# The two gate products of a decoder trunk: eight block products each before, seven after, with weight sums put aside in DRAM

## The reference, cut to what matters

```
hid  = square(relu(x @ ffn_w1[i]))
x    = layer_norm(ALPHA * x + hid @ ffn_w2[i], ln2_g[i], ln2_b[i])
gate = sigmoid(x @ ple_gate_w[i])          # 1024x1024 @ 1024x1024
x    = x + gate * (p[i] @ ple_w[i])        # 1024x256  @ 256x1024
```

## Time and profile before

| | |
|---|---|
| three runs, median (lowest to highest) | 2071.39 us (2070.79 to 2071.64) |
| the profiled execution, its own time | 2070.66 us |
| its span in the profile | 2068.9 us |
| PE busy | 2052.1 us (99%) |
| DVE, ACT, POOL busy | 1325.2, 853.9, 790.2 us |
| mean granted TensorE clock | 0.999 |
| moved by DMA | 306 MB, 148 GB/s |

### The profile page before, as it was taken

One profiled execution on the slowest core, in us unless ns is written; L12 is line 12 of the kernel. 1 busy time (PEld: TensorE's weight loads), 2 busy tenths in 40 slices (PEclk: granted clock), 3 DMA queues, 4 the chain that ended last, 5 costly groups with the idle time before them and its releaser, 6 DMA issues. The chain is left out here.

```text
span 2068.9 us, 25147 instructions
## 1 busy us (share of the span) xinstructions
PE 2052.1 (99%) x9437; PEld 1702.7 (82%) x9437; DVE 1325.2 (64%) x1677; ACT 853.9 (41%) x1241; POOL 790.2 (38%) x523
## 2 busy tenths in 40 slices
PE   9999999999999999999999999999999999999999
PEld 9888788888888888888878887888888888888887
DVE  4744775655666757564687769775655666666563
ACT  3112465454544334431433334655445543334430
POOL 5212157787702000212266751167877412000220
PEclk9999999999999999999999999999999999999999
DMA  5111123444589655411022238034444599554221
GB/s 189 42 62 45 38 82 137 144 161 156 197 309 390 218 201 182 141 34 41 21 88 86 87 133 299 1 122 145 150 158 142 205 382 362 185 202 153 97 87 41
DMA packets 190708, 306.05 MB, mean 148 GB/s; under 512 B 13472, under 2 KB 71932, under 8 KB 190588
## 3 DMA queue, kind: packets, MB, share of 16 engines
q1 hardware_dynamic: 189888, 304.14, 42.1%
q10 hardware_dynamic: 700, 0.31, 0.1%
HBM read 233.62 MB, written 70.78 MB: 147 GB/s over the span
## 5 line engine op out<-in xcount | busy, mean ns | idle before, releaser
L1326 POOL TENSOR_TENSOR w_lo<-raw,w_hi 128x512 fp32r<-128x512 f32 x92 | 131.0, 1455 | 744.0 <-ACT w_hi L1441 744.0
L1339 POOL TENSOR_TENSOR op_lo<-op_sum,op_hi 128x512 fp32r<-128x512 f32 x151 | 225.1, 1506 | 34.4 <-ACT op_hi L1643 28.5
L1608 ACT CAST hop_hi<-h_raw 128x1024 fp32r<-128x1024 f32 x124 | 130.4, 1051 | 257.0 <-PE bank_a L2367 155.4
L1643 ACT CAST op_hi<-op_sum 128x512 fp32r<-128x512 f32 x151 | 93.9, 622 | 329.5 <-POOL op_sum L1420 87.9
L2365 PE MATMUL bank_a<-wop_hi,hop_hi 128*128 128x512 f32 x576 | 224.2, 389 | 4.7 <-DVE resid L2153 4.7
L2131 DVE TENSOR_TENSOR hop_lo<-h_raw,hop_hi 128x1024 fp32r<-128x1024 f32 x124 | 152.0, 1226 | 117.5 <-ACT hop_hi L1608 117.3
L2367 PE MATMUL bank_a<-wop_hi,hop_lo 128*128 128x512 f32 x576 | 224.1, 389 | 0.0
L2366 PE MATMUL bank_a<-wop_lo,hop_hi 128*128 128x512 f32 x576 | 224.1, 389 | 0.0
L1339 POOL TENSOR_TENSOR op_lo<-w_raw,op_hi 128x512 fp32r<-128x512 f32 x115 | 164.2, 1428 | 116.4 <-ACT op_hi L1643 115.3
L2367 PE MATMUL bank_a<-xt_hi,op_lo 128*128 128x512 f32 x456 | 177.4, 389 | 0.0
L2365 PE MATMUL bank_a<-xt_hi,op_hi 128*128 128x512 f32 x456 | 177.4, 389 | 0.0
(11 more groups left out here) (243 smaller groups left out, 4879.4 us busy)
## 6 DMA issues: line engine op xcount, KB each, us to landing
w_raw<-in_ffn_w_dram SPq DMA_DIRECT2D x144, 512.0 KB, 6.8
h_raw<-h_spill SPq DMA_DIRECT2D x112, 512.0 KB, 5.2
h_spill<-h_tile SPq DMA_DIRECT2D x170, 256.0 KB, 2.1
w_raw<-in_ffn_w_dram SPq DMA_DIRECT2D x112, 256.0 KB, 3.3
w_raw<-in_od_w_in_dram SPq DMA_DIRECT2D x40, 256.0 KB, 3.3
w_raw<-in_od_w_out_dram SPq DMA_DIRECT2D x18, 512.0 KB, 7.6
raw<-in_ple_gate_w_dram SPq DMA_DIRECT2D x32, 256.0 KB, 3.5
h_spill<-h_tile2t SPq DMA_DIRECT2D x28, 256.0 KB, 2.0
```

Of the source, the lines that this page charges most:

```text
L1326: pool.tensor_tensor(lo, raw[:, n % NRAW, :], hi.bitcast(F32), ALU.subtract).then_inc(lo_split, 1)
L1339: pool.tensor_tensor(by_four(op_lo[s]), operand_raw(tr, b, op), by_four(op_hi[s]).bitcast(F32), ALU.subtract).then_inc(op_low, 1)
L1608: act.copy(hop_hi[k][:, :, :], h_raw[a.hop_chunk(i)][:, :, :]).then_inc(ahead_hi, 1)
L1643: act.copy(by_four(op_hi[s]), operand_raw(tr, b, op)).then_inc(op_high, 1)
```

## The change

The 1024x1024 gate product is cut in quadrants: tokens by input channels (A11, A12, A21, A22), input by output channels (B11 to B22). With S1 = A21+A22, S2 = S1-A11, S3 = A11-A21, S4 = A12-S2 and T1 = B12-B11, T2 = B22-T1, T3 = B22-B12, T4 = T2-B21 there are seven products: m1 = A11 B11, m2 = A12 B21, m7 = S3 T3, m6 = S2 T2, m5 = S1 T1, m3 = S4 B22, m4 = A22 T4. Each is 4 token tiles of 12 matmuls. The four output quadrants are sums of them, partly formed by letting a product run on in the same bank, partly by an ACT copy and a DVE addition. `p @ W_p` keeps its count, in four quadrants of four tiles (6 matmuls each): one among m2's tiles, the others (`p12`, `p22`, `p21`) at the end.

The operands made of weights (B22, T3, T1, T2, T4) are formed in the MLP's second product, in stages `park` beside items 20 to 47: ACT issues DMA loads of the weight quadrants, POOL makes the four sums, ACT casts to hi, DVE subtracts to lo, ACT issues the DMAs that put both into DRAM (`gate_dram`). In the gate stage SP loads each operand (2 MB: hi and lo, 1 MB each) when the product before it in the same buffer is done. The operands made of tokens (S1 to S4, A22) are formed by DVE and ACT within the gate stage. p's transposes now all stand after item 53, and p's load after item 47.

```diff
+GATE_ITEMS = ("m1", "m2", "m7", "m6", "m5", "m3", "m4", "p12", "p22", "p21")
+PARKED = ("B22", "T3", "T1", "T2", "T4")
+PARK_FROM, PARK_STEPS = 20, 14
...
-            if i == LAST_FORM - PAIRS:
+            for m in range(2):
+                s = i - PARK_FROM - m * PARK_STEPS
+                if 0 <= s < PARK_STEPS:
+                    add("park", item=s, half=m, layer=layer)
+            if i == LAST_FORM:
                 add("p", layer=layer)
...
-            if i == LAST_FORM + 4:
-                add("turn_p", half=0, layer=layer)
             if i == LAST_FORM + 5:
                 add("second", layer=layer)
+                add("turn_p", half=0, layer=layer)
+                add("turn_p", half=1, layer=layer)
...
     (SP, the loads in the gate stage)
+                if name == "m1":
+                    gate_product_done(sp, st, "m1")
+                    part("T3", 0)
+                if name == "m2":
+                    sp.wait_ge(b_full, st.gb + HT + 1)
+                    part("T2", 1)
+                if name == "m7":
+                    gate_product_done(sp, st, "m7")
+                    part("T1", 0)
...
+                if name == "m6":
+                    gate_product_done(sp, st, "m6")
+                    part("B22", 1)
+                if name == "m5":
+                    gate_product_done(sp, st, "m5")
+                    part("T4", 0)
...
     (POOL, one of three places of park)
+                if st.item == 4:
+                    park_landed(pool, st, 3)
+                    park_done(pool, st, "T3r")
+                    step(park[1], park[1], park[2], ALU.subtract)
+                    park_done(pool, st, "T1r")
+                    step(park[2], park[0], park[2], ALU.add)
...
     (ACT, the loads and stores of park, first steps)
+                if s == 0:
+                    if m == 0:
+                        act.wait_ge(ahead_dve, ahead[layer].dve[3 * PAIRS - 1])
+                    else:
+                        park_stored(act, st, 0)
+                    quarter(1, 1, park[0])
+                    quarter(0, 1, park[1])
+                if s == 2:
+                    park_done(act, st, "B22l")
+                    store("B22", 2, 3)
+                if s == 3:
+                    park_stored(act, st, 1)
+                    quarter(0, 0, park[2])
...
     (DVE, the operands of tokens behind m2; pairs of 128x1024)
+                if name == "m7":
+                    gate_product_done(dve, st, "m2")
+                    x_step(g_part, xt12[0].bitcast(F32), g_sum[48], ALU.subtract, "S2r")
+                    gate_x_done(dve, layer, "S4a1")
+                    x_low(xt11[1], g_sum[48], xt11[0], "S2")
+                    x_step(g_sum[168], g_sum[168], g_sum[176], ALU.add)
...
+                    x_step(g_sum[56], g_part, xt12[1].bitcast(F32), ALU.add, "S4a")
+                    x_low(xt12[1], g_sum[56], xt12[0], "S4")
+                if name == "m6":
+                    gate_product_done(dve, st, "m7")
+                    x_low(s3[1], g_sum[168], s3[0], "S1")
+                    affine(range(HT, HT + 2))
...
     (PE, m1 with the second half's transposes within)
+                if name == "m1":
+                    pe.wait_ge(unit_lo, st.need_x[0])
+                    for k in range(HT):
+                        if k == HT - 1:
+                            turn_groups(st.inner[0], range(0, 4))
+                        gate_tile(k, free_bank("A", st, k)).then_inc(a_full, 1)
+                    turn_groups(st.inner[0], range(4, 8))
+                    return
...
+                if name[0] == "m":
+                    x_part, w_part = {"m7": ("S3l1", "T3"), "m6": ("S2l1", "T2"), "m5": ("S1l1", "T1"),
+                                      "m3": ("S4l1", "B22"), "m4": ("Xl1", "T4")}[name]
+                    gate_x_done(pe, layer, x_part)
+                    gate_part_landed(pe, layer, w_part)
+                    for k in range(HT):
+                        gate_tile(k, free_bank(ring, st, k)).then_inc(full, 1)
+                    return
```

More of the change, by code:

```diff
@@ L388, in make_plan, with slab_pieces @@
     ends = {}
+    def slab_pieces(slab):
+        return 6 if slab[0] == "gate" and slab[2] else 4
     def add(kind, slab=None, last=False, **args):
@@ L580, in gates @@
         add("more", slab=("gate", layer, 0), split_next=False, load_next=False)
[L581 to L598 removed]
+        first = add("gm", item=0, layer=layer)
+        gx = add("gx", source="ln", half=1, js=list(range(KT)), layer=layer, ln=2 * layer + 1, ring="B")
+        first.inner = [gx]
+        turned[1] = "gb", at["gb"]
+        items = [first]
+        for i in range(1, len(GATE_ITEMS)):
+            if GATE_ITEMS[i] == "p21" and layer == 0:
+                nested = turns("gate", 0, [0, 1, 2, 3], nested=True)
+            args = dict(slab=("gate", layer, 1)) if i == 1 else {}
+            items.append(add("gm", item=i, layer=layer, load_next=GATE_ITEMS[i] == "m4",
+                             split_next=GATE_ITEMS[i] == "p22", **args))
+            if GATE_ITEMS[i] in ("m4", "p22"):
+                slab_end.append(("gb", at["gb"]) if GATE_ITEMS[i] == "m4" else ("ga", at["ga"]))
+        if layer == 0:
+            items[-1].inner = [nested]
+            turns("gate", 0, [4, 5, 6, 7])
+        for st in items:
+            st.heads = {GATE_ITEMS[s.item]: s for s in items}
+            st.gx = gx
+        gx.heads = items[0].heads
     def short_conv():
@@ L944, in staged @@
         def staged(st, k):
[L946 removed]
+            early = st.source == "ln" and st.ln % 2 == 0 or st.source == "gate"
+            if st.kind == "turn" and st.source == "gate" and st.half == 0 and st.js[k] >= 4:
+                return g_turn[:, st.js[k] - 4, :]
             if st.kind == "turn" and early and st.js[k] < 4:
@@ L1301, in stage @@
                     load_gb(ln1_g[0], ln1_b[0], D)
-                if st.kind == "gate" and st.layer == 1:
-                    c = slice(st.col * HALF, (st.col + 1) * HALF)
-                    for k, t in enumerate(st.tiles):
-                        sp.wait_ge(x_new, st.xnew + k + 1)
-                        sp.dma_start(out_v[:, t, c], resid[:, t, c]).then_inc(out_done, 16)
             for st in plan:
@@ new lines, in gate_units @@
+            def gate_units(st):
+                act.wait_ge(unit_lo, st.unit)
+                for k, j in enumerate(st.js):
+                    act.wait_ge(b_full, st.gb + k + 1)
+                    g = ROW_G[1] + st.layer * KT + j
+                    b = ROW_B[1] + st.layer * KT + j
+                    act.activation(g_sum[168 if j < 4 else 176][:, j % 4, :], bank_b[(st.gb + k) % RING][:, :], ACT.Identity,
+                                   scale=cols[:, g:g + 1], bias=cols[:, b:b + 1]).then_inc(gate_turned, 1)
@@ L1555, in stage @@
                     split_high(st.cur + 1, st.piece, 4, end)
-                fifth = st.split_next and st.cur + 1 < n_slabs and slabs[st.cur + 1][0][0] == "gate"
                 if st.kind == "split":
@@ L2408, in stage @@
             def stage(st):
-                if st.first and st.cur > 0 and not (st.kind == "more" and slabs[st.cur][0][2] >= 2):
+                if st.first and st.cur > 0:
                     pe.wait_ge(lo_split, st.n("piece"))
```

502 lines of the change are left out of this document (376 added, 126 removed).

## The result

The changed kernel takes 2075.26 us (median of 20 runs, 2072.83 to 2080.68) against 2071.66 (20 runs, 2070.32 to 2073.14): ratio 1.0021, 95% interval 1.0014 to 1.0027. It is slightly slower; 2057.2 had been forecast, in a range up to 2067. The profiled execution took 2075.14 us, its span is 2073.6.

A forecast was written before the change was run, and what follows sets the result against it. PE, busy 99% of the span, was taken to bound the kernel: 21.8 us of matmuls saved less 7.6 us of new PE waits leaves 14.2, so 2057.2 us against 2071.39; range 2049.5 to 2067.

The forecast's parts named there:

- What bounds the kernel, and what goes: Whole kernel: PE, busy 99%, bounds it; 48 fewer gate matmuls a layer at 0.227 us save 21.8 us in both layers.
- Parking in the second product, "I take 0": MLP's second product, items 20 to 47: idle time and prepared items hide the parking steps, so PE loses 0 us.
- the prediction's own sign of it: MLP's second product: a stretch grown longer than 305 us would show the forecast wrong, parking not being hidden.
- four prepared items (21.8 us) between it and PE: MLP's second product: operands prepared four items ahead were counted as 21.8 us of cover for ACT's load and store waits.
- The port: MLP's second product: POOL's sums may each hold DVE 2.46 us on the shared port; DVE stays under 88 us, sum unchanged.
- Rival 3: MLP's second product: load and store round trips of 12.5 us outrun DVE's cover, 9.6 us reach PE, 2066.8; chance 0.15.
- Before m1: Ahead of the first gate product: the norm ends later, PE waits 0.3 us a layer, bounds 0 and 2.5.
- The gate stage: Gate stage, each layer: PE waits for DVE's low parts, 0.5 us for S2 ahead of m6, 2.0 for S1 ahead of m5.
- The weight operands: Gate stage: 2 MB loads land in about 10 us, shortest time allowed 10.9, so PE waits 0; bounds 7 and 19.
- rival 2: Gate stage: weight operands land late, at 19 us a part costing 14.2 us a layer, 2085.6; chance 0.09.
- The end of layer 0: Mixer's first product: POOL's splits slow three DVE additions by 0.9 us, so PE waits 1.5 us for xt_lo; bounds 0 and 5.
- The end of the program: After the last matmul: DVE's last two operations follow as before, plus 0.5 us.

The follow-up runs named there:

- e1: Changed kernel with every parking step cut to 128 of 1024 columns or 64 KB, gate-stage loads of parked operands too: 2057.47 us, ratio 0.9934 to before.
- e3: Changed kernel with DVE's five parking subtractions of each half cut to 128 of 1024 columns: 2059.16 us, ratio 0.9941 to before.
- e2: Changed kernel with only GpSimd's four parking sums of each half cut to 128 of 1024 columns: 2061.43 us, ratio 0.9951 to before.
- e10: Changed kernel with only the second half's parking begun at item 33 instead of 34: 2082.89 us, ratio 1.0050 to before.
- e11: Changed kernel with bank readings at items 24 and 48 earlier, second-half parking from item 33, sums on DVE, POOL's layer-0-end splits held back: 2056.74 us.
- e9: Changed kernel with DVE's bank readings at items 24 and 48 put ahead of one item's operand work: 2061.95 us, ratio 0.9946 to before.

## Why the prediction was wrong, step by step

- *What bounds the kernel, and what goes.* Right: PE, 96 matmuls, 0.227 us each, 21.8 us. e1 ends within 0.3 us of the forecast.
- *Parking in the second product, "I take 0".* **This step failed.** It measured 9.2 and 8.8 us, and the prediction's own sign of it came: a second product longer than 305 us, here 313.8. It set the new work against two covers: DVE's idle time (27 us a half) and "four prepared items (21.8 us) between it and PE". Both are true of the operands, and no operand was late. But the same queue holds the reading of m7's banks, which PE needs about an item after the bank is full and which has 0.5 us. The idle time in front of it was also no reserve: in the 52 us ahead of item 47 and up to the reading, before, DVE was idle 14.2 us, 5.8 for loads and 8.4 for ACT. Of this 6.3 was left afterwards, the last of it 16.9 us ahead of the reading. An average over 88 us did not tell that. Of the new work DVE's own subtractions (e3) and POOL's sums (e2) delay the reading; stores can too (e10), and what they cost in the changed kernel is open.
- *The port.* The prediction gave POOL's sums 2.46 us each and said that the sum does not change by them. They took 3.1 on average (group of instructions by line, which answers to the earlier trace rows),

```profile
L1477 POOL TENSOR_TENSOR park<-park,park 128x1024 f32<-128x1024 f32 x16 | 49.8, 3111 | 248.3 <-DMA park<-in_ple_gate_w_dram 142.1
```

  and of the 13 DVE instructions of 128x1024 that began while one ran, ten took 3.4 us instead of 1.22 and three 2.2 to 2.6. The Trainium skill, "SBUF — State Buffer", Who interferes with whom, has the rule (an exclusive lock between DVE and GpSimd); the trace agrees, 3.42 against 1.22 us. The prediction cited the rule and set it against the average over 88 us.
- *Rival 3, "parking is not hidden".* The right place and kind, at 0.15. Its size was wrong, 9.6 us in all against 18, as it too counted the lead of 21.8 us as cover, and nothing in it spoke of the clock (5.2 of the 18).
- *Before m1.* Forecast 0.3 a layer; PE waits for the norm in neither layer.
- *The gate stage.* The second wait, for S1, was forecast at 2.0 and measured 1.46; the first, for S2, at 0.5 and measured 0.29. Timeline of PE:

```profile
934.77 0.50 PE L2730 MATMUL bank_a<-w_hi,xt_hi 128*128 128x512 f32 x1 [0.29 <-DVE xt_lo L2223]
...
947.40 0.50 PE L2730 MATMUL bank_a<-w_hi,xt_hi 128*128 128x512 f32 x1 [1.46 <-DVE xt_lo L2223]
...
1008.71 0.50 PE L2730 MATMUL bank_a<-xt_hi,w_hi 128*128 128x512 f32 x1 [2.72 <-DVE xt_lo L2037]
```

- *The weight operands.* Right, and rival 2 falls: no wait for them. The page's section 6, which answers to the earlier trace rows, has 1 MB landing 4.8 and 7.0 us after issue:

```profile
gate_parts<-park_r ACTq DMA_DIRECT2D x40, 512.0 KB, 4.7
w_hi<-gate_parts SPq DMA_DIRECT2D x10, 1024.0 KB, 4.8
w_lo<-gate_parts SPq DMA_DIRECT2D x10, 1024.0 KB, 7.0
```

- *The end of layer 0.* Right in place and cause, 2.72 us against 1.5, but by other instructions: the forecast had three additions slowed by 0.9 us each, and POOL's splits made two casts take 2.90 us instead of 0.76 (e11) and two additions 1.0 instead of 0.7. e11 shows the cause. *The end of the program*: 0.5 forecast, 0.53 measured.

The measured terms other than the parking come to 4.5 us in layer 0 (4.3 forecast) and 2.3 in layer 1 (3.3). That e1 ends so near the forecast is in part luck: the missing 0.3 before m1, the shorter waits in the gates and the longer one at layer 0's end nearly cancel. So one term of 0 that should have been 18 turned 14 us of gain into 4 of loss.

## What to carry to other kernels

Before work is called hidden on an engine that works in order, list everything that stands in its queue, and find the item with the least slack: beside operands with 20 us of lead there may be the release of a bank with 0.5. That slack is read from two starts, the releasing instruction's and the released one's. Where a new job must go onto such an engine, first put the tight instruction ahead of the work that has lead (here worth 13 us between the medians of e9 and the changed kernel), and then look at what its move pushes back, and beside which load a moved store comes to stand.
